# Reciprocal roots of the norms: logarithm and exponential of ScalarE replaced by a bit estimate and three Newton steps on VectorE

## The chip, the cores and the metric

One core of a Trainium2 chip runs the whole program: TensorE (PE), VectorE (DVE), ScalarE (ACT), GpSimd (POOL) and SyncE (SP), which issues nearly all transfers. The metric is the device time of one execution in microseconds (us); lower is better.

## The reference, cut to what matters

Two transformer blocks over 1024 tokens of width 1024, in float32. Every norm needs one reciprocal root for each token:

```python
def layer_norm(x, g, b):      # ln0 on the input, ln1 after the mixer, ln2 after the feed-forward block
    mu = xf.mean(-1, keepdims=True)
    var = jnp.square(xf - mu).mean(-1, keepdims=True)
    return ((xf - mu) * lax.rsqrt(var + EPS) * g + b)
def rmsnorm(x, g):            # norm_mix, norm_cross, norm_mem, norm_mlp, norm_final
    return xf * lax.rsqrt(jnp.mean(xf * xf, axis=-1, keepdims=True) + NORM_EPS) * g

x = layer_norm(x, ln0_g, ln0_b); mod = silu(c) @ w_ada + b_ada
y = hybrid_mixer(h, ...)                                # ends in @ w_o
x = layer_norm(ALPHA * x + (1.0 + gt_a) * y, ln1)
y = conv_ffn(h, ...)                                    # up, convolution, silu gate, down
x = layer_norm(ALPHA * x + (1.0 + gt_f) * y, ln2)
h = h + concat(attn, rec)(rmsnorm(h, norm_mix)) @ w_out
h = h + memory_cross_attention(rmsnorm(h, norm_cross), rmsnorm(mem, norm_mem), ...)   # ends in @ w_co
h = h + square(relu(rmsnorm(h, norm_mlp) @ w_mlp_in)) @ w_mlp_out
out = rmsnorm(h, norm_final)
```

## The kernel before, in words

The tokens lie in eight tiles of 128 rows; `resid` holds them. A list of units (`schedule`) is written once, and every engine walks through the whole list in that order and does its own part of each unit. Each engine therefore has one queue whose order is the order of the list. Between engines there are only named waits on semaphores: an instruction that waits stops everything behind it on its engine, whether or not that needs the same value. Where a unit has no part on an engine, the engine passes it at once.

A norm of a group of tiles is `norm_start`: for each tile `moments` (VectorE, the layer norms `s` = 0, 1, 2) or `squares` (ScalarE, the others), and then one unit `deviation` for the group. `deviation` turns the variances, one column for each tile (so 2, 3, 4 or 8 columns of 128 rows), into the reciprocal roots `rstd`. VectorE writes variance plus EPS (L1576, counted as "var"), ScalarE waits for it and does `Ln` (L2290) and `Exp` with scale -0.5 (L2292), VectorE waits for that and does one Newton step in four small instructions (L1579, L1581, L1583, L1585). There are 17 such units. After them come the users: `norm_apply` on VectorE (L1601 for ln1; L1605 and L1609 for ln2) or on ScalarE (L2337 writes `xhat`), `final` (L2342 on ScalarE, then L1658 on VectorE and the store), the transposes of `norm_features` (L1092 on TensorE) and their evictions (L1639, L1646, L1631 on VectorE, L2305 and L2314 on ScalarE). Of ln2, GpSimd adds the bias row (L2709), which is counted as `rows_added`.

Where other work stands near a `deviation`, in the order of the list:

- After the last group of `w_o` (tiles 6 and 7): `deviation(1, 6)`, then the product with `w_ada` for the second gate in eight steps (L1068), its copies `ada_out` on ScalarE (L2362, tile `mod_last`), its turn on TensorE (L1080), then `ahead`, at which ScalarE takes the first three panels of the feed-forward weights apart (`halve`, L2253, after the panel has landed) and GpSimd makes their low parts (`lower`, L2639), then the features of tiles 6 and 7, of which GpSimd makes the odd low parts, and then `up`.
- At the end of `down`: `deviation(2, 0)`, `squares` of the memory tokens (L2328 on `mem_t`), `deviation(norm_mem)`, the eight last evictions of `down` (L1979), the memory's features, `ck` (L1438, copied by ScalarE at L2582) with the first tiles' `norm_apply` between, the moments of tiles 4 to 7, `deviation(2, 4)`, `ck(2)`, `squares` of norm_mix for tiles 0 to 3, `deviation(norm_mix, 0)`, `norm_apply` of ln2 for tiles 4 to 7 (L1605, L1609), `cv`, and the features of tiles 0 to 3 (L1092, L1646). A softplus of eight columns (`rg_params`: L1752 on VectorE, `Exp` L2393 and `Ln` L2395 on ScalarE) stands before `ck`.
- `norm_cross` in `w_out`, `norm_mlp` in `w_co` (three groups each, with features of one group between the products of the next), and `norm_final` behind the last two halves of `mlp_out`.

ScalarE's functions live in tables that an instruction ACT_TABLE_LOAD brings in; it stands before the wait of the function that needs it. Copy and Square appear in the trace without a load of their own.

The tiles `panel_hi` (three buffers) share addresses with `xhat` 0 and 1, whose last readers before the feed-forward block are the transposes of tiles 4 and 5 and `norm_scale_rows` of tile 5 (L1615, `rows_applied`). Weights go through six slots, loaded in order by SyncE as the slots come free (L2836).

Of the kernel before, what the change touches and what calls it, by code (L numbers as in the profile page):

```python
# [8 lines left out]
I32 = mybir.dt.int32  # L9
ALU = mybir.AluOpType  # L10
ACT = mybir.ActivationFunctionType
# [4 lines left out]
D = 1024  # L16
KD = D // P
T = 1024
NT = T // P
HALVES = T // BANK  # L20
EPS = 1e-6
# [1471 lines left out]
def vector_program(k):  # L1493
    dve = k.nc.vector
    v = Program(k, dve)
# [71 lines left out]
    def deviation(s, n0, n1):  # L1567
        centred = s in (0, 1, 2)
        if centred:
            v.wait_ge("moments", s, n1 - 1)  # L1570
        else:
            v.wait_ge("squares", s, n1 - 1)
        cols = slice(n0 + NT, n1 + NT) if s == "norm_mem" else slice(n0, n1)
        var = k.moments[:, cols, 1 if centred else 0]
        x, y, step = k.newton[:, 0, cols], k.rstd[:, cols], k.newton[:, 1, cols]
        dve.tensor_scalar(x, var, 1.0 if centred else 1.0 / D, EPS, ALU.mult, ALU.add).then_inc(  # L1576
            *v.new("deviation_dve", s, n0, "var"))
        v.wait_ge("deviation_act", s, n0, "exp")
        dve.tensor_tensor(step, y, y, ALU.mult).then_inc(*v.new("deviation_dve", s, n0, 1))  # L1579
        v.wait_ge("deviation_dve", s, n0, 1)  # L1580
        dve.tensor_tensor(step, step, x, ALU.mult).then_inc(*v.new("deviation_dve", s, n0, 2))  # L1581
        v.wait_ge("deviation_dve", s, n0, 2)
        dve.tensor_scalar(step, step, -0.5, 1.5, ALU.mult, ALU.add).then_inc(*v.new("deviation_dve", s, n0, 3))  # L1583
        v.wait_ge("deviation_dve", s, n0, 3)
        dve.tensor_tensor(y, y, step, ALU.mult).then_inc(*v.new("deviation_dve", s, n0, 4))  # L1585
        v.wait_ge("deviation_dve", s, n0, 4)

    def ln0_norm(n):
        dve.tensor_scalar(k.xhat0[:, n, :], k.x_in[:, n, :], k.moments[:, n, 0:1], k.rstd[:, n:n + 1], ALU.subtract,
# [624 lines left out]
    def mlp_out(i, u, h, p, tiles):  # L2214
        for n in tiles:
            v.wait_ge(*v.filled("mlp_out", i, u, h, n))
            if u or i:
# [4 lines left out]
    v.run(dict(norm_scale_rows=norm_scale_rows, unit_length=unit_length, barrier=barrier, constants=constants, vectors=vectors, ada_turn=ada_turn, piece_out=piece_out, ln0_norm=ln0_norm,  # L2222
               ln0_resid=ln0_resid, gla_start=gla_start, z_gate=z_gate, gg_gate=gg_gate,
               modulation=modulation, norm_rows=norm_rows, moments=moments, deviation=deviation, norm_apply=norm_apply,
               norm_features=norm_features, final=final, project=project, to_tokens=to_tokens, decay_gates=decay_gates,
               delta_start=delta_start, delta=delta, gla_gates=gla_gates, gla=gla, ffn_taps=ffn_taps, up=up, down=down,
# [7 lines left out]
def scalar_program(k):  # L2234
    act = k.nc.scalar
    a = Program(k, act)
# [3 lines left out]
    def halve(p):  # L2240

        at = k.split_index[p]
        if at >= SPLITS:
            a.wait_ge(*k.released(a, splits[at - SPLITS]))
        if k.panel_list[p][3] is not None:
            a.wait_ge("panel_scaled", p)
        else:
            a.wait_ge("panel_loaded%d" % (p % SLOTS), p)
        if k.panel_list[p][0] == "up":
            for c in range(4):  # L2250
                for h in range(HALVES):
                    a.wait_ge("z_gated", c, h)
        act.activation(k.halves_of(p)[0], k.view(p), ACT.Copy).then_inc(*a.new("halved_hi", p))  # L2253

    def before(index, used):
        if used is None or not k.panel_list[used][2]:
            return
        while split_turn[0] < len(splits) and split_turn[0] <= k.split_index[used] + SPLITS - 1 and \
                same_group(k, splits[split_turn[0]], used) and k.passed(splits[split_turn[0]], SPLITS, index) and \
                k.passed(splits[split_turn[0]], None, index):  # L2260
            halve(splits[split_turn[0]])
            split_turn[0] += 1
# [18 lines left out]
    def condition():  # L2281
        for n in range(k.n_vt):
            a.wait_ge(*a.evicted("vectors", n))
        act.activation(k.cond[:], k.col("c", 0, KD), ACT.Silu).then_inc(*a.new("condition_silu"))

    def deviation(s, n0, n1):
        cols = slice(n0 + NT, n1 + NT) if s == "norm_mem" else slice(n0, n1)
        x, y = k.newton[:, 0, cols], k.rstd[:, cols]
        a.wait_ge("deviation_dve", s, n0, "var")
        act.activation(y, x, ACT.Ln).then_inc(*a.new("deviation_act", s, n0, "ln"))  # L2290
        a.wait_ge("deviation_act", s, n0, "ln")
        act.activation(y, y, ACT.Exp, scale=-0.5).then_inc(*a.new("deviation_act", s, n0, "exp"))  # L2292

    def norm_features(s, tiles, chunks):
        cols = slice(tiles[0] * P, (tiles[-1] + 1) * P)
# [302 lines left out]
    def mlp_in(i, c, h, p):  # L2598
# [4 lines left out]
        if i:  # L2603
# [2 lines left out]
        act.activation(k.mlp_hid[c][0][:, half(h)], k.mlp_sq[h][:], ACT.Copy).then_inc(*a.new("mlp_hi", i, c, h))  # L2606

    a.run(dict(unit_length=unit_length, barrier=barrier, vectors=vectors, condition=condition, ada_out=ada_out, conv_silu=conv_silu,
               piece_out=piece_out, z_gate=z_gate, gg_gate=gg_gate, rab=rab, deviation=deviation, squares=squares,
               norm_apply=norm_apply, norm_features=norm_features, final=final, project=project, decay_gates=decay_gates, delta=delta, gla_gates=gla_gates, gla=gla,  # L2610
               up=up, rg_params=rg_params, rg_in=rg_in, rglru=rglru, masks=masks, weights=weights, turn=turn,
               merge=merge, out_turn=out_turn, ck=ck, c_score=c_score, c_finish=c_finish, mlp_in=mlp_in))
# [382 lines left out]
def build(nc, dram, known):  # L2995
    with ExitStack() as stack:
        k = Shared(nc, dram, known, stack)
        sync_program(k)
        tensor_program(k)
        vector_program(k)  # L3000
        scalar_program(k)
        gpsimd_program(k)
        return k.signals.seen
# [35 lines left out]
```

## Time and profile before

| what | value |
|---|---|
| median of 3 runs | 3252.06 us (3250.96 to 3254.82) |
| the profiled execution | 3255.33 us, of which 3254.1 us are the span of its instructions |
| TensorE busy | 3083.5 us (95%) |
| VectorE, ScalarE, GpSimd busy | 1450.2, 963.9 and 734.8 us |
| mean granted clock of TensorE | 0.978 |

Busy time is a sum over the span and says nothing of order; what sets the end is read from the chain that ended last and from the timeline. In rows of a timeline the first number is the start in us from the span's start, the second the time from there to the end of the merged instructions, and the square bracket is how long the engine had been idle and who released it.

### The profile page before, as it was taken

How to read it: one execution, taken by the hardware profiler on the slowest of the kernel's cores; microseconds unless marked ns; L12 is line 12 of the kernel's file. 1: busy time of each engine (PE TensorE's matmuls, PEld its weight loads, DVE VectorE, ACT ScalarE, POOL GpSimd, SP SyncE). 2: the span in 40 equal slices, each digit the busy share in tenths (PEclk: the TensorE clock that was granted, in tenths of full speed). 3: DMA queues.
4: the chain of work that ended last, by engine and by line, in shares of the span. 5: the costliest groups of instructions: out<-in, count | busy, mean ns of one | idle time of the engine just before them, and what ended most of it. 6: DMA issues, size and time to landing. Idle time of an engine off the chain costs nothing.

```text
span 3254.1 us, 31713 instructions
## 1 busy us (share of the span) xinstructions
PE 3083.5 (95%) x12748; PEld 2101.5 (65%) x12748; DVE 1450.2 (45%) x2248; ACT 963.9 (30%) x1516; POOL 734.8 (23%) x467
## 2 busy tenths in 40 slices
PE   6999999999979999999987999999998999999997
PEld 3444467675437888888864444586443788888886
DVE  7245443332555545455555544673132333333334
ACT  2246622223022222222224540263334322222123
POOL 3011012220234444444432111100000122222220
PEclk9999999999989999999998999999999999999998
DMA  7210012213231111111122112002301111111111
GB/s 254 65 27 25 26 48 77 64 28 115 97 103 52 59 52 46 46 52 46 46 65 65 39 38 62 19 3 62 102 26 33 35 50 46 52 46 52 46 52 52
DMA packets 197649, 185.12 MB, mean 57 GB/s; under 512 B 16103, under 2 KB 147583, under 8 KB 197503
## 3 DMA queue, kind: packets, MB, share of 16 engines
q1 hardware_dynamic: 196928, 182.89, 18.0%
q8 instruction: 102, 1.67, 0.2%
q14 instruction: 44, 0.36, 0.0%
q10 hardware_dynamic: 575, 0.20, 0.0%
HBM read 171.24 MB, written 9.70 MB: 56 GB/s over the span
## 4 chain that ended last, share of the span: by engine, by line
PE 84%; DVE 7%; ACT 6%; issue 1%; POOL 1%; DMA 1%; ACTq 0%; DVEq 0%; SPq 0%; POOLq 0%
PE bank L1099 63%; PE bank L1125 6%; PE bank L1419 2%; PE bank L1189 1%; PE bank L1230 1%; PE bank L1244 1%; PE bank L1092 1%; PE bank L1253 1%; PE bank L1403 1%; PE bank L1068 1%; PE bank L1373 1%; PE bank L1395 1%; DVE ffn_conv L1968 1%; DVE ffn_conv L1964 1%; PE bank L1392 1%
## 5 line engine op out<-in xcount | busy, mean ns | idle before, releaser
L1099 PE MATMUL bank<-ft,panel 128*128 128x512 f32 x832 | 361.2, 595 | 1.8 <-ACT sq_inv L2457 1.0
L2639 POOL TENSOR_TENSOR panel_lo<-panel,panelm_hi 128x1024 fp32r<-128x1024 f32 x64 | 153.2, 2394 | 812.1 <-ACT panelm_hi L2253 812.1
L1099 PEld LDWEIGHTS bank<-ft,panel 128*128 128x128 f32 x832 | 158.4, 191 | 201.2 <-issue 201.2
L1125 PE MATMUL bank<-ft,panel 128*128 128x512 f32 x576 | 271.6, 609 | 7.4 <-ACT mod_part L2362 4.8
L1099 PE MATMUL bank<-ft_hi,panel_lo 128*128 128x512 f32 x704 | 277.4, 394 | 0.0
L1099 PE MATMUL bank<-ft_hi,panel_hi 128*128 128x512 f32 x704 | 276.5, 393 | 0.0
L1099 PE MATMUL bank<-ft_lo,panel_hi 128*128 128x512 f32 x704 | 276.3, 393 | 0.0
L1964 DVE TENSOR_SCALAR ffn_conv<-ffn_in,ffn_taps 128x512 f32<-128x512 f32 x88 | 115.4, 1312 | 296.3 <-ACT ffn_in L2502 296.3
L2220 DVE TENSOR_TENSOR resid<-resid,bank 128x512 f32<-128x512 f32 x256 | 174.5, 686 | 151.6 <-PE bank L1099 150.7
L2639 POOL TENSOR_TENSOR panel_lo<-panel,panel_hi 128x1024 fp32r<-128x1024 f32 x66 | 158.1, 2404 | 251.2 <-ACT panel_hi L2253 251.2
L1099 PE MATMUL bank<-ftm_hi,panelm_hi 128*128 128x512 f32 x512 | 200.5, 392 | 0.0
L1099 PE MATMUL bank<-ftm_lo,panelm_hi 128*128 128x512 f32 x512 | 200.1, 391 | 0.0
L1099 PE MATMUL bank<-ftm_hi,panel_lo 128*128 128x512 f32 x512 | 199.9, 390 | 0.0
L1099 PE MATMUL bank<-panelm_hi,mlp_hid_hi 128*128 128x512 f32 x512 | 199.2, 389 | 0.0
L1099 PE MATMUL bank<-panel_lo,mlp_hid_hi 128*128 128x512 f32 x512 | 199.2, 389 | 0.0
L1099 PE MATMUL bank<-panelm_hi,mlp_hid_lo 128*128 128x512 f32 x512 | 199.2, 389 | 0.0
L1125 PEld LDWEIGHTS bank<-ft,panel 128*128 128x128 f32 x576 | 105.3, 194 | 114.0 <-issue 110.8
L1099 PE MATMUL bank<-panel,mix 128*128 128x512 f32 x384 | 168.6, 596 | 0.9 <-DVE mix L2199 0.9
L1968 DVE SCALAR_TENSOR_TENSOR ffn_conv<-ffn_in,ffn_taps,ffn_conv 128x512 f32<-128x512 f32 x176 | 156.5, 889 | 6.2
L1099 PEld LDWEIGHTS bank<-ft_lo,panel_hi 128*128 128x128 f32 x704 | 132.6, 188 | 30.9
L1099 PEld LDWEIGHTS bank<-ft_hi,panel_hi 128*128 128x128 f32 x704 | 132.6, 188 | 29.6
L1099 PEld LDWEIGHTS bank<-ft_hi,panel_lo 128*128 128x128 f32 x704 | 132.6, 188 | 29.4
(421 smaller groups left out, 5325.1 us busy)
## 6 DMA issues: line engine op xcount, KB each, us to landing
panel<-in_w_in SPq DMA_DIRECT2D x52, 512.0 KB, 3.7
panel<-in_w_ada SPq DMA_DIRECT2D x48, 512.0 KB, 3.9
panel<-in_ffn_w_up SPq DMA_DIRECT2D x44, 512.0 KB, 3.7
panel<-in_w_mlp_in SPq DMA_DIRECT2D x32, 512.0 KB, 3.9
panel<-in_w_mlp_out SPq DMA_DIRECT2D x32, 512.0 KB, 3.5
panel<-in_w_o SPq DMA_DIRECT2D x24, 512.0 KB, 3.5
panel<-in_w_out SPq DMA_DIRECT2D x24, 512.0 KB, 3.5
panel<-in_ffn_w_down SPq DMA_DIRECT2D x22, 512.0 KB, 3.5
```

What stands on the lines that cost most here:

```text
L1068: m = te.matmul(ps[rows, :], k.cond[:, c:c + 1].broadcast_to([P, 32]), w[:, kk, :], start=(c < 4), stop=(c >= 4))
L1092: m = te.transpose(ps[:, tile(i)], src[:, tile(j)], k.ident[:])
L1099: m = te.matmul(ps, a, b, start=(start and j == 0), stop=(stop and j == len(pairs) - 1))
L1125: m = te.matmul(ps[:], w[0][:, kk, :], k.ft[:, kk, half(h)], start=(kk == 0), stop=(kk == KD - 1))
L1189: m = te.matmul(ps[:, tile(h)], lhs(h), rhs_of(h), start=True, stop=True)
L1230: m = te.matmul(ps[:, h * GC:(h + 1) * GC], t.ltm[:, h, :], blocks(t.inv, lv, 0)[:, h], start=True, stop=True)
L1244: m = te.matmul(ps[:, h * GC:(h + 1) * GC], t.prod[:, h, :], blocks(t.inv_t, lv, 1)[:, h], start=True, stop=True)
L1419: m = te.matmul(ps[:, at:at + HD + 1], k.p_t[(2 * t + hb) % 4][:, 2 * side + c, :], v, start=(hb == side == c == 0), stop=(hb == side == c ...
L1964: dve.tensor_scalar(out, pre[:, 1 + h * BANK:1 + (h + 1) * BANK], w[:, 0:1], w[:, 3:4], ALU.mult, ALU.add).then_inc(*v.new("ffn_tap", c, g ...
L1968: dve.scalar_tensor_tensor(out, pre[:, 1 + j + h * BANK:1 + j + (h + 1) * BANK], w[:, j:j + 1], out, ALU.mult, ALU.add).then_inc(*v.new("f ...
L2220: evict(dve.tensor_tensor(r, r, v.bank("mlp_out", i, u, h, n)[:], ALU.add), "mlp_out", i, u, h, n)
L2639: pool.tensor_tensor(lo, k.view(p), hi.bitcast(F32), ALU.subtract).then_inc(*g.new("halved_lo", p))
```

## The change

ScalarE's part of `deviation` is gone. VectorE makes the whole of it: the variance, its word shifted right by one, the first estimate as a constant minus that word (both on int32 views of the same tiles), and then three Newton steps of three instructions, each of which counts a semaphore and is waited for by the next. The last still counts as `("deviation_dve", s, n0, 4)`, which the users wait for. ScalarE's `halve` gets two named waits for the panels of `up`: the last transposes of tiles 4 and 5, and `rows_applied` of tile 5.

```diff
-        dve.tensor_scalar(x, var, 1.0 if centred else 1.0 / D, EPS, ALU.mult, ALU.add).then_inc(
-            *v.new("deviation_dve", s, n0, "var"))
-        v.wait_ge("deviation_act", s, n0, "exp")
-        dve.tensor_tensor(step, y, y, ALU.mult).then_inc(*v.new("deviation_dve", s, n0, 1))
...
-        dve.tensor_tensor(y, y, step, ALU.mult).then_inc(*v.new("deviation_dve", s, n0, 4))
-        v.wait_ge("deviation_dve", s, n0, 4)
+        def did(ins, *what):
+            ins.then_inc(*v.new("deviation_dve", s, n0, *what))
+            v.wait_ge("deviation_dve", s, n0, *what)
+        did(dve.tensor_scalar(x, var, 1.0 if centred else 1.0 / D, EPS, ALU.mult, ALU.add), "var")
+        did(dve.tensor_scalar(step.bitcast(I32), x.bitcast(I32), 1, None, ALU.logical_shift_right), "halved")
+        did(dve.tensor_scalar(y.bitcast(I32), step.bitcast(I32), -1.0, float(0x5F3759DF), ALU.mult, ALU.add), "first")
+        for n in range(1, 4):
+            did(dve.scalar_tensor_tensor(step, y, -0.5, y, ALU.mult, ALU.mult), "square", n)
+            did(dve.tensor_tensor(step, step, x, ALU.mult), "product", n)
+            did(dve.scalar_tensor_tensor(y, step, 1.5, y, ALU.add, ALU.mult), *(("step", n) if n < 3 else (4,)))
...
                 for h in range(HALVES):
                     a.wait_ge("z_gated", c, h)
+            a.wait_ge(*a.filled("feat", 1, 4, KD - 1))
+            a.wait_ge("rows_applied", 1, 5)
...
-    def deviation(s, n0, n1):
-        cols = slice(n0 + NT, n1 + NT) if s == "norm_mem" else slice(n0, n1)
-        x, y = k.newton[:, 0, cols], k.rstd[:, cols]
-        a.wait_ge("deviation_dve", s, n0, "var")
-        act.activation(y, x, ACT.Ln).then_inc(*a.new("deviation_act", s, n0, "ln"))
-        a.wait_ge("deviation_act", s, n0, "ln")
-        act.activation(y, y, ACT.Exp, scale=-0.5).then_inc(*a.new("deviation_act", s, n0, "exp"))
```

## Rows read from the trace of the kernel before

**Rows 1.** The page, part 4: the chain that ended last, by engine.
```profile
PE 84%; DVE 7%; ACT 6%; issue 1%; POOL 1%; DMA 1%; ACTq 0%; DVEq 0%; SPq 0%; POOLq 0%
```

**Rows 2.** ScalarE's groups by line: xcount | busy us, mean ns | idle before.
```profile
L2292 ACT ACT_TABLE_LOAD x17 | 21.8, 1283 | 0.3
L2290 ACT ACT_TABLE_LOAD x16 | 20.5, 1283 | 0.3
```

**Rows 3.** Timeline of the last 31 us, both groups of norm_final.
```profile
3223.34 0.17 DVE L1576 TENSOR_SCALAR newton<-moments 128x4 f32<-128x4 f32 x1 [1.27 <-ACT square L2328]
...
3228.41 4.63 DVE L1658 TENSOR_TENSOR resid<-resid,norm_rows 128x1024 f32<-128x1024 f32 x4 [1.27 <-ACT resid L2342]
...
3232.96 4.87 DVE L2220 TENSOR_TENSOR resid<-resid,bank 128x512 f32<-128x512 f32 x8
...
3241.08 0.17 DVE L1576 TENSOR_SCALAR newton<-moments 128x4 f32<-128x4 f32 x1 [3.26 <-ACT square L2328]
...
3244.12 0.16 DVE L1579 TENSOR_TENSOR newton<-rstd 128x4 f32<-128x4 f32 x1 [2.86 <-ACT rstd L2292]
...
3244.91 4.27 ACT L2342 ACTIVATE resid<-resid,rstd 128x1024 f32<-128x1024 f32 x4 [0.83 <-DVE rstd L1585]
```

**Rows 4.** VectorE's timeline: one instruction on int32 words, one small two-operation form.
```profile
54.95 0.43 DVE L2093 TENSOR_SCALAR dist_i<-dist_i 128x512 int32<-128x512 int32 x1
...
1711.96 0.17 DVE L1752 SCALAR_TENSOR_TENSOR lam<-lam_sp,lam 128x8 f32<-128x8 f32 x1
```

**Rows 5.** Timeline from 931 to 953 us, end of w_o: SyncE, ScalarE, VectorE, TensorE, GpSimd.
```profile
931.60 0.47 SPq L2836 DMA_DIRECT2D panel<-in_ffn_w_up  x1
...
938.52 0.20 ACT L2290 ACTIVATE rstd<-newton 128x2 f32<-128x2 f32 x1 [13.16 <-DVE newton L1576]
...
944.92 2.95 ACT L2253 ACTIVATE panel_hi<-panel 128x1024 fp32r<-128x1024 f32 x3
...
938.32 0.17 DVE L1576 TENSOR_SCALAR newton<-moments 128x2 f32<-128x2 f32 x1
...
941.06 1.53 DVE L1601 TENSOR_SCALAR xhat<-resid,moments,rstd 128x1024 f32<-128x1024 f32 x2
...
940.76 2.07 PE L1080 MATMUL bank<-mod_last,quads 128*128 128x512 f32 x2 [6.11 <-ACT mod_last L2362]
...
946.05 7.15 POOL L2639 TENSOR_TENSOR panel_lo<-panel,panel_hi 128x1024 fp32r<-128x1024 f32 x3 [14.20 <-ACT panel_hi L2253]
```

**Rows 6.** Transfers issued from 930 to 931.7 us: KB each, us to landing.
```profile
panel<-in_ffn_w_up SPq DMA_DIRECT2D x1, 512.0 KB, 7.9
```

**Rows 7.** Timeline from 1682 to 1765 us: SyncE, ScalarE, VectorE, GpSimd, TensorE.
```profile
1682.63 0.37 SPq L2978 DMA_DIRECT2D mem_t<-in_mem  x1
...
1697.11 0.21 ACT L2290 ACTIVATE rstd<-newton 128x4 f32<-128x4 f32 x1 [14.57 <-DVE newton L1576]
...
1698.74 1.04 ACT L2328 ACTIVATE square<-mem_t 128x1024 f32<-128x1024 f32 x1
...
1704.91 4.87 DVE L1979 TENSOR_TENSOR resid<-resid,bank 128x512 f32<-128x512 f32 x8
...
1745.00 0.81 DVE L1605 TENSOR_SCALAR resid<-resid,moments,rstd 128x1024 f32<-128x1024 f32 x1
...
1728.59 2.36 POOL L2709 TENSOR_TENSOR resid<-resid,norm_rows 128x1024 f32<-128x1024 f32 x1 [1.16 <-DVE resid L1609]
...
1761.02 3.68 PE L1092 MATMUL bank<-ident,xhat 128*128 128x128 f32 x16 [8.66 <-DVE ft L1646]
```

**Rows 8.** Transfers issued from 1680 to 1700 us.
```profile
mem_t<-in_mem SPq DMA_DIRECT2D x1, 1024.0 KB, 4.9
```

**Rows 9.** Chain of waits from 2255 to 2390 us (w_out, norm_cross), by line.
```profile
by line: PE bank L1099 94.1%; PE bank L1092 5.2%; DVE ft L1646 0.7%; issue 0.1%; DVEq L93 0.0%
```

**Rows 10.** TensorE's timeline in w_co, behind norm_mlp's second unit.
```profile
2495.70 1.97 PE L1092 MATMUL bank<-ident,xhat 128*128 128x128 f32 x8 [5.74 <-DVE ftm_lo L1631]
```

**Rows 11.** Stretch by engine: us, busy (instructions) of five engines, PEclk, DMA share, GB/s.
```profile
2496.00:2498.00 2.00, 2.00 (x9) 1.80 (x8) 0.66 (x2) 0.98 (x2) 0.00 (x0) 0.50 0.00 0
```

More of the change, by code:

```diff
@@ L1575, in deviation @@
         x, y, step = k.newton[:, 0, cols], k.rstd[:, cols], k.newton[:, 1, cols]
-        dve.tensor_scalar(x, var, 1.0 if centred else 1.0 / D, EPS, ALU.mult, ALU.add).then_inc(
-            *v.new("deviation_dve", s, n0, "var"))
-        v.wait_ge("deviation_act", s, n0, "exp")
-        dve.tensor_tensor(step, y, y, ALU.mult).then_inc(*v.new("deviation_dve", s, n0, 1))
[L1580 to L1584, printed above, removed]
-        dve.tensor_tensor(y, y, step, ALU.mult).then_inc(*v.new("deviation_dve", s, n0, 4))
-        v.wait_ge("deviation_dve", s, n0, 4)
+        def did(ins, *what):
[8 more added lines that the diff above has]
+            did(dve.scalar_tensor_tensor(y, step, 1.5, y, ALU.add, ALU.mult), *(("step", n) if n < 3 else (4,)))
     def ln0_norm(n):
@@ L2608, in scalar_program @@
     a.run(dict(unit_length=unit_length, barrier=barrier, vectors=vectors, condition=condition, ada_out=ada_out, conv_silu=conv_silu,
-               piece_out=piece_out, z_gate=z_gate, gg_gate=gg_gate, rab=rab, deviation=deviation, squares=squares,
+               piece_out=piece_out, z_gate=z_gate, gg_gate=gg_gate, rab=rab, squares=squares,
                norm_apply=norm_apply, norm_features=norm_features, final=final, project=project, decay_gates=decay_gates, delta=delta, gla_gates=gla_gates, gla=gla,
```

## The prediction

> **What bounds the kernel now.** I read the page's chain of waits first: TensorE holds 84% of it, VectorE 7% and ScalarE 6% [rows 1]. So most of the time is products, and the change can win only in the stretches where TensorE stands still for a norm. The second view is ScalarE's groups by line, for the number of table loads: 16 for `Ln`, 17 for `Exp`, 1.283 us each [rows 2], so two for nearly each of the 17 units. Third, the timeline around every `deviation`, to see two things: how long VectorE takes from the variance (L1576) to the first user, and what stands behind ScalarE's wait in its queue. Fourth, the chain in each stretch, for whether a norm is on it at all.
>
> The 17 units fall into two kinds. In nine of the eleven norms that ScalarE's squares feed, ScalarE is busy until the variance is ready and both loads are exposed: from L1576 to the first user 3244.91 - 3241.08 = 3.83 us [rows 3] (the other two of the eleven, norm_mem and the first of norm_mix, take nearly the same, since their squares too end just before). In those fed by VectorE's moments (six; ln0, with eight columns and its `Ln` table late, lies between) ScalarE has waited idle, has its `Ln` table in already, and the way takes 941.06 - 938.32 = 2.74 us [rows 5].
>
> **Part 1: the new sequence.** Twelve small dependent instructions on VectorE. The pitch of dependent small ones is (3244.91 - 3244.12)/4 = 0.20 us, with the wait between them in it [rows 3]. The kinds: a two-operation form with three operands on eight columns takes 0.17 us, as the others do [rows 4]. A form on int32 words has no small row; 512 columns take 0.43 us [rows 4], so for 2 to 8 columns it lies between 0.20 (the small float ones) and 0.43. I take 0.20, as the instruction is of the same kind and only the columns differ. Sum 12 x 0.20 = 2.40 us; with the upper bound for two of them 2.86. Against 3.83 that is a gain of 1.43 us (bounds 0.97 to 1.43; nothing below 0.20 is likely, as each waits for the one before), against 2.74 a gain of 0.34 (bounds -0.12 to 0.34). I call these the long and the short gain.
>
> The Trainium skill, page "VectorE: DVE Perf Modes", section "The DRAIN you can't avoid", says that chaining does not help, that the next instruction waits for the pipeline to empty, and that one should make the count of instructions small. That speaks against going from five to twelve. By its formula for a float two-input instruction, (N+151)/0.96 ns (same page, errata section), twelve would make an estimated 1.94 us before any gap; the trace's 0.20 us pitch is what I use, and by either the count costs less than the loads give back.
>
> **Part 2: where the gain is on the path.** ln0: the chain there runs over transfers of `w_ada` and TensorE alone; gain 0, the cover is those transfers. norm_cross, three units: the chain from 2255 to 2390 us holds TensorE for 99% and no norm [rows 9]; gain 0, the next group's products hide it, and without them it would be 1.43 each. norm_mlp, three units: the first lies under products, but behind the second TensorE stands 5.74 us until VectorE evicts a transpose (L1631), which is queued behind `deviation` [rows 10], and behind the third the pattern repeats (5.9 us). ScalarE's half of that eviction also stood behind the loads and comes earlier still. Gain 2 x 1.43 = 2.9 us. norm_final, two units: in the first, the users L1658 hold VectorE until 3232.96, when the eight last evictions start, all but the last of whose banks TensorE has long filled; they in turn set the second squares. So both units are in the chain, the second with nothing beside it [rows 3]. Gain 2 x 1.43 = 2.9 us.
>
> **Part 3: what stood behind ScalarE's waits.** This is the larger part. ScalarE waited in five units for VectorE's variance. Two places have other work behind that.
>
> (a) End of `w_o`. The first two groups of ln1 are short ones on the chain, 2 x 0.34 = 0.7 us. In the third ScalarE waits 13.16 us until 938.52 [rows 5]. Behind it stands the copy `mod_last`, whose input is older than TensorE's last work before it stops at 940.76 - 6.11 = 934.65; TensorE is idle from there to 940.76 for that copy [rows 5]. Then come the second copy and the three `panel_hi` (944.92), and GpSimd's three `panel_lo` (946.05, 7.15 us), behind which its part of the features is queued and for that TensorE [rows 5]. With the wait gone, TensorE turns the first half at about 934.7 (1.0 us at full clock), the last two steps of the product are done at about 938.5, as their panels land at about 937, and the second copy ends at about 939. Late next is the first `up` panel: issued at 931.60 and 7.9 us on the way, so 939.5 [rows 5, 6]. One `panel_hi` is 2.95/3 = 1.0 us, so GpSimd starts at 940.6 instead of 946.05, and with the 0.7 us of the groups before at 939.9. The place gives 6.1, say 6.0 us in all. Bounds: 1.0 us if the copy is not what holds it (three short gains), 7 if the panels land sooner. VectorE's own way (`xhat` 941.06 + 1.53, the two gate rows and `feat_part`, now shifted to about 943.3) ends before GpSimd's (947.1), so it is covered. The new waits of `halve` name things that are long done: GpSimd adds tile 5's row after L1615, which stands behind that group's features in VectorE's queue, and GpSimd was through with it at 946.05 - 14.20 = 931.85 [rows 5], over 7 us before the first `panel_hi` can start. They cost nothing; if they did, ScalarE's features of tiles 6 and 7 behind them would be late next.
>
> (b) End of `down`. ScalarE waits 14.57 us until 1697.11, does `Ln` and `Exp`, and only then, at 1698.74, the squares of `mem_t` [rows 7], though the memory landed at 1682.63 + 0.4 + 4.9 = 1687.9 [rows 7, 8]. Without the wait these are done by about 1690.5 (two of 1.25), and on VectorE the two units follow each other: 1696.9 + 2.4 + 2.4 = 1701.7. The eight evictions L1979 then start at 1701.7 instead of 1704.91: 3.2 us [rows 7]. After that the softplus: its `Exp` found its table in, left by the norm; now the silu table is in and a load of 1.28 us comes before it, of which ScalarE's idle 1.0 us hides most. Cost 0.3 us, so 2.9 us remain. The same pattern stands at 1734.2, 2 of 2 here: ScalarE waits 13.5 us for ln2's second group, and the four squares of norm_mix for tiles 0 to 3 follow only from 1736.3. Their inputs are complete with GpSimd's L2709 at 1728.59 + 2.36 = 1730.95, now 1728.1 [rows 7]; the last square, 1.25 us, ends at 1729.3, before VectorE's ln2 variance at 1731.3. So VectorE does the two units back to back, 1731.3 + 2.4 + 2.4 = 1736.1, and L1605 starts there instead of at 1745.00: 8.9 us [rows 7]. From L1605 to TensorE's transposes at 1761.02, for which TensorE had stood 8.66 us on VectorE's `ft`, is one queue of VectorE [rows 7], so TensorE goes on 8.9 us sooner. TensorE's `cv`, itself 3 us sooner, ends at about 1738, in time. The second norm_mix unit is hidden by the products of `rg` and gives 0. Bounds: 3.5 us (two long and two short gains) if the squares don't run ahead, 9.6 with the softplus free.
>
> **Part 4: loads.** 33 loads leave ScalarE. Of them the exposed ones are counted above. A few later functions now bring a table in themselves (the softplus above); the first silu of the feed-forward block loses its load. The Trainium skill, page "ScalarE: Activation LUTs", section "What ACT_TABLE_LOAD costs", gives 1283 ns for the load and about 1380 ns of drain on top for every switch. The trace agrees on the first [rows 2] and shows no drain: `Ln` starts at 1.28 us behind its load. By the page's 2.66 us a long unit would have lasted over 6 us, and it lasts 3.83.
>
> **Sum.** (a) 6.0 + (b) 8.9 + norm_mlp 2.9 + norm_final 2.9 = 20.7 us. The profiled execution goes from 3255.33 to 3234.6, and the median, 3.3 us lower, from 3252.06 to 3231.4 us (0.64%). A measurement of this kernel tells about 0.2%, 6.5 us, from no change.
>
> **The rivals.**
> 1. Only the latencies count: the work behind ScalarE's waits is held by something else (the panels' landing, GpSimd, banks). Then (a) gives 1.0 and (b) 3.5, the sum is 1.0 + 3.5 + 5.8 = 10.3 and the time 3242. For it: in (a) 3 MB of panels are in flight. Against it: the rows put the released work's inputs 6 to 10 us ahead. Between it and the forecast lie the cases with one of the two places whole. Together 0.22.
> 2. No change, within 6.5 us: the gains are absorbed by feed-forward and later products, which wait for panels. Against: TensorE's waits name VectorE and ScalarE, not a transfer, except at `w_ada`. 0.05.
> 3. Slower: the instructions on int32 words are slow in the small form. To decide, the long units (mlp, final: 4) and the pairs in (b) would have to lose the 20.7 us; with 11 units on the path that is 1.9 us for each unit, 0.95 us for each of two instructions over the 0.20 us. At 1.5 us each the sum is 20.7 - 11 x 2.6 = -8 us, 3260 us. Against it: 0.43 us for 512 columns [rows 4]. 0.03.
> The forecast has 0.70.
>
> **Clock.** TensorE's granted clock falls in these waits: behind the 5.74 us of rows 10 it is 0.50, the lower level of 1.2 GHz, for the products from 2496 to 2498 [rows 11], against 0.978 in the mean. I count no gain from it, as 4.3 us of that wait stay (5.74 - 1.43). Where a fall is avoided, products of some 3 to 4 us take half, an estimate of 1.5 us a place, for three places about 5 us. This sets the lower end: 3226. The upper end reaches past rival 1 to 3243. Faster 0.92, same 0.05, slower 0.03.
>
> **What the profile after would show.** No ACT_TABLE_LOAD under `deviation`; L1576 to the first user 2.4 us everywhere; `mod_last` before 935 and `panel_lo` before 941; squares of `mem_t` at 1688 less the shift, L1979 and L1605 3 and 9 us sooner relative to the last product of `down`'s first half; norm_cross without effect; from the last matmul to the end 2.8 us less. Wrong it would be if a panel or GpSimd, not ScalarE's queue, ends TensorE's wait in (a), or if the last L2220 waits for TensorE.

## The result, and the profile after

The changed kernel takes 3236.98 us in the median of 6 runs (3233.82 to 3239.71), the kernel before 3253.44 us in 6 runs beside them. The ratio is 0.9947, with a 95% interval of 0.9937 to 0.9957: 17.2 us less by the ratio (16.5 by the medians), where 20.7 had been forecast. The predicted time was 3231.4, its range 3226 to 3243. The profiled execution took 3237.97 us with a span of 3236.7.

**The new sequence.** VectorE's timeline of the kernel after, last unit of norm_final, which answers to [rows 3], with ScalarE's first user of the root at the end:

```profile
3225.16 0.17 DVE L1583 TENSOR_SCALAR newton<-moments 128x4 f32<-128x4 f32 x1 [3.26 <-ACT square L2325]
3225.36 0.17 DVE L1584 TENSOR_SCALAR newton<-newton 128x4 int32<-128x4 int32 x1
3225.57 0.17 DVE L1585 TENSOR_SCALAR rstd<-newton 128x4 int32<-128x4 int32 x1
3225.77 0.16 DVE L1587 SCALAR_TENSOR_TENSOR newton<-rstd 128x4 f32<-128x4 f32 x1
...
3227.35 0.16 DVE L1589 SCALAR_TENSOR_TENSOR rstd<-newton,rstd 128x4 f32<-128x4 f32 x1
...
3227.55 4.27 ACT L2339 ACTIVATE resid<-resid,rstd 128x1024 f32<-128x1024 f32 x4 [2.42 <-DVE rstd L1589]
```

Read the starts: they are 0.20 us apart, also from one instruction on int32 words to the next. From the variance to the first user it is 3227.55 - 3225.16 = 2.39 us, before 3.83. The two-sided question on the int32 form (0.20 or up to 0.43) is settled at the lower end. ScalarE loads 102 tables in place of 136.

**End of w_o.** Timeline of the kernel after, 931 to 955 us, the rows that answer to [rows 5]: ScalarE, VectorE, GpSimd, TensorE:

```profile
931.26 0.59 ACT L2359 COPY mod_last<-bank 128x512 f32<-128x512 f32 x1 [7.54 <-PE bank L1068]
938.77 0.59 ACT L2359 COPY mod_last<-bank 128x512 f32<-128x512 f32 x1 [6.93 <-PE bank L1068]
939.25 1.06 ACT L2258 ACTIVATE panel_hi<-panel 128x1024 fp32r<-128x1024 f32 x1
940.62 1.06 ACT L2258 ACTIVATE panel_hi<-panel 128x1024 fp32r<-128x1024 f32 x1 [0.30 <-DMA panel<-in_ffn_w_up]
...
937.98 0.17 DVE L1583 TENSOR_SCALAR newton<-moments 128x2 f32<-128x2 f32 x1
...
940.36 5.67 DVE L1604 TENSOR_SCALAR xhat<-resid,moments,rstd 128x1024 f32<-128x1024 f32 x2
945.95 2.37 DVE L1950 COPY ffn_taps<-cols 128x132 f32<-128x132 f32 x1
...
949.56 0.98 DVE L1642 TENSOR_SCALAR feat_part<-bank,in_scale,in_bias 128x256 f32<-128x256 f32 x2
...
940.39 7.84 POOL L2636 TENSOR_TENSOR panel_lo<-panel,panel_hi 128x1024 fp32r<-128x1024 f32 x3 [8.87 <-ACT panel_hi L2258]
951.07 0.72 POOL L2715 TENSOR_TENSOR ft_lo<-feat_part,ft_hi 128x256 fp32r<-128x256 f32 x1 [2.83 <-ACT ft_hi L2302]
...
954.74 0.78 PE L1099 MATMUL bank<-ft_hi,panel_hi 128*128 128x512 f32 x1
```

ScalarE does what was forecast: the copy goes ahead of the norm, and the panels' high parts follow as they land. GpSimd starts its low parts at 940.39, 5.66 us sooner than in [rows 5], or 5.3 us when both are measured from the variance. But VectorE's two `xhat` instructions, which started within 0.03 us of it, now take 5.67 us in place of 1.53, and the copy of the taps behind them 2.37. So the features come late, GpSimd waits 2.83 us for them, and `up` starts 16.76 us behind the variance, where it was 18.52.

**End of down.** The same timeline, 1684 to 1750 us (ScalarE, VectorE, TensorE), for [rows 7]:

```profile
1684.69 1.06 ACT L2325 ACTIVATE square<-mem_t 128x1024 f32<-128x1024 f32 x1 [6.41 <-DMA mem_t<-in_mem]
...
1705.73 1.28 ACT L2390 ACT_TABLE_LOAD   x1
...
1725.92 1.06 ACT L2325 ACTIVATE square<-resid 128x1024 f32<-128x1024 f32 x1 [2.36 <-POOL resid L2706]
...
1699.84 4.87 DVE L1982 TENSOR_TENSOR resid<-resid,bank 128x512 f32<-128x512 f32 x8
...
1749.93 3.68 PE L1092 MATMUL bank<-ident,xhat 128*128 128x128 f32 x16 [8.88 <-DVE ft L1649]
```

The squares of `mem_t` now stand right behind their transfer, 14 us sooner than in [rows 7] (12.2 us measured from ln2's variance), and those of norm_mix are done at 1727.1, before ln2's variance at 1729.13. The softplus brings its own table in (L2390), as foreseen.

**Where the time came from.** Each column is the time in us from one instruction to the next: `g0` to `g2` are the variances of ln1's three groups, `up` is TensorE's first product of it, `2a` and `2b` are ln2's variances, `mix` the second one of norm_mix, `cross` the first of norm_cross, `m1` to `m3` those of norm_mlp, `f1` and `f2` those of norm_final. The numbers at the left are those of the experiments below. It is worked out from the starts of L1583 (L1576 with the logarithm) and of L1099 in the profiled executions of this and the later kernels:

```
              start   g0-g1  g1-g2  g2-up   up-2a  2a-2b 2b-mix mix-cross cross-m1 m1-m2 m2-m3  m3-f1  f1-f2 f2-end
before       862.27   41.73  34.32  18.52  740.06  37.28  36.04   502.60   204.52 13.73 25.39  706.88  17.74  13.01
after        864.52   39.67  33.79  16.76  740.34  34.05  29.99   502.77   204.51 13.73 23.06  705.67  16.30  11.58
5 again      860.69   39.67  33.76  16.57  740.44  34.05  29.99   502.81   204.52 13.73 23.07  705.67  16.31  11.57
1 wait all   862.92   39.66  33.77  19.50  739.21  36.74  34.93   500.52   204.51 13.73 25.08  706.73  16.31  11.56
2 wait ln1   863.30   39.66  33.78  19.50  739.24  34.24  29.98   500.52   204.51 13.73 23.28  705.80  16.31  11.55
3 hold       862.99   39.66  33.77  14.86  740.11  34.23  29.98   500.52   204.53 13.73 23.42  705.94  16.30  11.58
4 hold,first 857.83   41.36  34.22  10.47  740.55  34.05  29.98   502.65   204.51 13.74 24.68  706.88  16.30  11.56
6 two steps  863.19   39.07  33.50  16.22  739.37  32.89  28.54   500.53   204.51 13.73 22.69  705.62  15.71  10.98
7 five steps 862.82   42.28  34.36  17.90  739.94  36.74  32.37   502.97   204.52 13.73 25.45  706.90  17.49  12.77
8 4 and 6    861.89   39.07  33.36   9.88  740.72  32.89  28.81   502.16   204.51 13.74 24.15  706.73  15.72  10.98
9 bef,first  862.51   40.03  33.77  14.94  739.77  37.30  36.04   502.55   204.51 13.73 25.37  706.84  17.75  13.03
```

From the first variance of ln1 to the end it is 3254.1 - 862.27 = 2391.8 us before and 2372.2 after: 19.6 us less. The first 860 us, in which little is changed, differ from one execution to the next by up to 6.7 us (857.8 to 864.5), and with them one profiled time from another. So the 17.2 us of the ratio (interval 14.0 to 20.5) and the stretches' 19.6 us do not contradict each other.

### The profile page after: what moved, and what is told of

Same layout as the page of the kernel before. It is cut to its first block, busy times and chain, and to the rows that moved or that the text cites. A ratio compares the mean times of both kernels' runs of the same rounds, so it can differ in the third digit from the quotient of the medians.

```text
span 3236.7 us, 31765 instructions
## 1 busy us (share of the span) xinstructions
PE 3081.1 (95%) x12748; PEld 2099.1 (65%) x12748; DVE 1475.7 (46%) x2367; ACT 913.9 (28%) x1448; POOL 735.5 (23%) x467
## 4 chain that ended last, share of the span: by engine, by line
PE 85%; DVE 7%; ACT 4%; issue 1%; DMA 1%; POOL 1%; SPq 0%; ACTq 0%; DVEq 0%; POOLq 0%
PE bank L1099 63%; PE bank L1125 6%; PE bank L1419 2%; PE bank L1189 1%; PE bank L1230 1%; PE bank L1244 1%; PE bank L1253 1%; PE bank L1403 1%; PE bank L1092 1%; PE bank L1373 1%; PE bank L1068 1%; PE bank L1395 1%; DVE ffn_conv L1971 1%; DVE ffn_conv L1967 1%; PE bank L1392 1%
## 5 line engine op out<-in xcount | busy, mean ns | idle before, releaser
L1099 PE MATMUL bank<-ft,panel 128*128 128x512 f32 x832 | 361.4, 595 | 1.8 <-ACT sq_inv L2454 1.0
L1099 PEld LDWEIGHTS bank<-ft,panel 128*128 128x128 f32 x832 | 158.5, 191 | 201.4 <-issue 201.4
L1099 PE MATMUL bank<-ft_hi,panel_lo 128*128 128x512 f32 x704 | 277.0, 393 | 0.0
L1099 PE MATMUL bank<-ft_hi,panel_hi 128*128 128x512 f32 x704 | 276.3, 392 | 0.0
L1099 PE MATMUL bank<-ft_lo,panel_hi 128*128 128x512 f32 x704 | 276.0, 392 | 0.0
L1099 PE MATMUL bank<-ftm_hi,panelm_hi 128*128 128x512 f32 x512 | 200.7, 392 | 0.0
L1099 PE MATMUL bank<-ftm_lo,panelm_hi 128*128 128x512 f32 x512 | 200.2, 391 | 0.0
L1099 PE MATMUL bank<-ftm_hi,panel_lo 128*128 128x512 f32 x512 | 200.1, 391 | 0.0
L1099 PE MATMUL bank<-panelm_hi,mlp_hid_hi 128*128 128x512 f32 x512 | 199.2, 389 | 0.0
L1099 PE MATMUL bank<-panel_lo,mlp_hid_hi 128*128 128x512 f32 x512 | 199.2, 389 | 0.0
L1099 PE MATMUL bank<-panelm_hi,mlp_hid_lo 128*128 128x512 f32 x512 | 199.2, 389 | 0.0
L1099 PE MATMUL bank<-panel,mix 128*128 128x512 f32 x384 | 167.7, 594 | 0.9 <-DVE mix L2202 0.9
L1099 PEld LDWEIGHTS bank<-ft_lo,panel_hi 128*128 128x128 f32 x704 | 132.4, 188 | 30.8
L2210 DVE TENSOR_TENSOR mlp_square<-mlp_act 128x512 f32<-128x512 f32 x64 | 44.3, 692 | 235.7 <-ACT mlp_act L2599 235.7
L1099 PEld LDWEIGHTS bank<-ft_hi,panel_lo 128*128 128x128 f32 x704 | 132.4, 188 | 29.4
```

Source lines behind the costliest of these rows:

```text
L1099: m = te.matmul(ps, a, b, start=(start and j == 0), stop=(stop and j == len(pairs) - 1))
L2210: dve.tensor_tensor(k.mlp_sq[h][:], k.mlp_act[h][:], k.mlp_act[h][:], ALU.mult).then_inc(*v.new("mlp_square", i, c, h))
```

## The experiments

**1. ScalarE waits again, in all norms.** It has its unit back, with a wait for the finished root and nothing else. The latency stays new, what stands behind the wait is held again.

```diff
+    def deviation(s, n0, n1):
+        a.wait_ge("deviation_dve", s, n0, 4)
```

> The changed kernel, with ScalarE again waiting in every norm until VectorE's reciprocal root is there (the last Newton step), but computing nothing. It parts the latency of the norms from what stands behind ScalarE's waits. The prediction's terms: the end of w_o falls from 6.0 to 1.0 us and the end of down from 8.9 to 3.5, so +10.4 us against the changed kernel's 3237, 3247. Read from the changed kernel's trace, where the third group of ln1 brought less than forecast, I expect +5.4 at the end of down and +2 to +3 at the end of w_o, so 3244 to 3246. Rival 1 (only the latencies count): no difference, 3237.

Measured: 3248.79 us, ratio 0.9982 (0.9973 to 0.9991), 11.4 us above the changed kernel by the two ratios, and more than the 3244 to 3246 us expected. Without what stood behind the waits some 6 us of the 17 are left (up to 1.7 us more, as the waits here end later, see below), and rival 1 falls. ScalarE's timeline of this kernel:

```profile
938.72 0.59 ACT L2362 COPY mod_last<-bank 128x512 f32<-128x512 f32 x1 [16.64 <-DVE rstd L1589]
...
1697.45 1.06 ACT L2328 ACTIVATE square<-mem_t 128x1024 f32<-128x1024 f32 x1 [17.77 <-DVE rstd L1589]
```

Both waits name the root, not data. In the table the end of down loses 2.69 + 4.94 = 7.6 us, not 5.4, and g2-up 2.7 to 2.9. Part of this is that the wait is for the last step, 2.4 us behind the variance, while before the squares of `mem_t` started 1.84 us behind it (1698.74 - 1696.90). That is 0.56 us for each of two pairs of norms, so about 6.5 of the 7.6 us are the queue's. TensorE's wait behind the second norm_mlp was 5.12 us in place of 4.29, too: ScalarE's half of the features counted there.

**2. The wait in ln1 alone.** As 1, with `if s == 1:` ahead of the wait.

> As the kernel before this one, but ScalarE waits in the three groups of ln1 alone. The prediction's term for the end of w_o: +5.0 us, 3242. By the changed kernel's trace, where up's first product came 16.8 us behind the variance and before the change 18.5: +2.3 us (the copy mod_last again 2.4 us behind the variance), 3239. If the place gave nothing through the queue: 3237. The end of down stays as in the changed kernel.

Measured: 3238.84 us, ratio 0.9951 (0.9939 to 0.9964). The time alone can't tell 2 us from none. The stretch can: g2-up is 19.50 as in 1, against 16.76 and 16.57, and all of 2a to mix stays as in the changed kernel. So freeing ScalarE at the end of w_o gives 2.8 us in the kernel as changed, not 5.3, and some 0.56 us of the 2.8 may again be the later end of this wait. The two places are independent of each other.

**3. GpSimd's first low part waits for VectorE's last `xhat`.**

```diff
         g.wait_ge("halved_hi", p)
+        if p == min(q for q, x in enumerate(k.panel_list) if x[0] == "up"):
+            g.wait_ge("normed", 1, 7)
         pool.tensor_tensor(lo, k.view(p), hi.bitcast(F32), ALU.subtract)...
```

> The changed kernel, but GpSimd starts the first up panel's low part only when VectorE has normalised tile 7. Theory (VectorE's float32 work from SBUF to SBUF stands still while GpSimd computes): the two xhat instructions take 1.5 us again instead of 5.67, the copy of the taps 0.23 instead of 2.37 or what of GpSimd still meets it, feat_part starts at about 944 instead of 949.56, GpSimd goes from its last panel_lo to ft_lo without the wait of 2.83, and up starts 1.3 to 2.8 us sooner in the stretch; total 3234 to 3236. Rival (VectorE is slowed by something else there, the transfers of the panels or ScalarE): xhat keeps 5.7 us, up starts up to 1.5 us later, 3237 to 3238.5.

Measured: 3236.2 us, ratio 0.9941 (0.9927 to 0.9954); the time alone can't tell this kernel from the changed one. VectorE and GpSimd of this kernel:

```profile
938.79 1.54 DVE L1604 TENSOR_SCALAR xhat<-resid,moments,rstd 128x1024 f32<-128x1024 f32 x2
940.25 0.23 DVE L1950 COPY ffn_taps<-cols 128x132 f32<-128x132 f32 x1
...
940.48 7.17 POOL L2638 TENSOR_TENSOR panel_lo<-panel,panel_hi 128x1024 fp32r<-128x1024 f32 x3 [10.51 <-DVE xhat L1604]
947.61 0.72 POOL L2717 TENSOR_TENSOR ft_lo<-feat_part,ft_hi 128x256 fp32r<-128x256 f32 x1
```

The same transfers are in flight and ScalarE does the same work beside it; only GpSimd is held. `xhat` has its 1.5 us back, the copy its 0.23, GpSimd goes on to the features without a wait, and `up` starts 14.86 us behind the variance although GpSimd began 1.7 us later relative to it. So it is GpSimd's work beside it that makes `xhat` slow.

**4. Only the first panel's low part ahead of the features.** As 3, and:

```diff
-        while turn[0] < len(worked) and turn[0] <= worked.index(used) + SPLITS - 1 and \
+        more = 0 if k.order[index][0] == "ahead" else SPLITS - 1
+        while turn[0] < len(worked) and turn[0] <= worked.index(used) + more and \
```

> As the kernel before this one, and GpSimd makes only the first up panel's low part ahead of the features, the next two behind them. Theory: GpSimd is through with its panel at about 944.4, the features' low parts are then paced by VectorE and ScalarE (1.9 us a pair, four pairs), up's first product at about 948 to 950 instead of 954.74, minus 5 to 7 us in this stretch, if the second panel's low part is in time; total 3231 to 3233. Rival: the low parts that now come behind the features meet VectorE's and TensorE's work there, or the second panel is late, and half or all of it is given back: 3234 to 3237.

Measured: 3232.86 us, ratio 0.9932 (0.992 to 0.9945). GpSimd and TensorE of this kernel:

```profile
937.47 2.36 POOL L2638 TENSOR_TENSOR panel_lo<-panel,panel_hi 128x1024 fp32r<-128x1024 f32 x1 [10.51 <-DVE xhat L1604]
940.21 0.72 POOL L2718 TENSOR_TENSOR ft_lo<-feat_part,ft_hi 128x256 fp32r<-128x256 f32 x1 [0.38 <-ACT ft_hi L2302]
...
947.43 5.74 POOL L2638 TENSOR_TENSOR panel_lo<-panel,panel_hi 128x1024 fp32r<-128x1024 f32 x2
...
943.88 0.78 PE L1099 MATMUL bank<-ft_hi,panel_hi 128*128 128x512 f32 x1
...
950.86 0.50 PE L1099 MATMUL bank<-ft_hi,panel_hi 128*128 128x512 f32 x1 [0.24 <-POOL panel_lo L2638]
```

`up` starts 10.47 us behind the variance, 6.1 to 6.3 sooner than in the changed kernel, and the second panel costs 0.24 us. By the ratios 4.6 us of it arrive (0.9946 - 0.9932), with intervals of 0.0025. The table says that nothing is lost behind it: up-2a is 740.55, against 740.34 and 740.44. What this profiled execution loses against the changed kernel stands in stretches that its edit doesn't touch: g0-g1 (1.7 us more than in the changed kernel), g1-g2 (0.4), m2-m3 (1.6) and m3-f1 (1.2). Experiment 5 looks at these.

**5. The changed kernel again.** No edit.

> The changed kernel unaltered, once more. Every theory: 3235 to 3239, ratio 0.994 to 0.996. What it tells: how far the first 860 us of one execution differ from another's (they were 2.3 us longer in the changed kernel's profiled execution than in the one before the change), and how much the first eight products behind the second norm_mlp vary with the granted clock behind one and the same wait of 4.29 us (4.1 to 5.7 us so far).

Measured: 3236.99 us, ratio 0.9946 (0.9934 to 0.9959). In the table this execution agrees with the first to 0.2 us in every stretch, but its start is 3.8 us shorter. Inside g2-up the agreement hides a difference. Here GpSimd began 2.07 us behind the variance, not 2.41, and met the last Newton instruction, of two columns, before `xhat`:

```profile
936.29 2.26 DVE L1589 SCALAR_TENSOR_TENSOR rstd<-newton,rstd 128x2 f32<-128x2 f32 x1
...
936.19 7.39 POOL L2636 TENSOR_TENSOR panel_lo<-panel,panel_hi 128x1024 fp32r<-128x1024 f32 x3 [8.53 <-ACT panel_hi L2258]
```

It took 2.26 us in place of 0.16, so the root of this group was there 4.43 us behind the variance, not 2.34. The 2.3 us by which the changed kernel's start had been longer in its profile are no effect of the change that can be shown. TensorE's timeline behind the second norm_mlp, in the changed kernel (first execution):

```profile
2483.30 1.97 PE L1092 MATMUL bank<-ident,xhat 128*128 128x128 f32 x8 [4.29 <-DVE ftm_lo L1634]
2485.07 4.08 PE L1099 MATMUL bank<-panel,mix 128*128 128x512 f32 x8
```

The same place in experiment 3:

```profile
2477.55 1.91 PE L1092 MATMUL bank<-ident,xhat 128*128 128x128 f32 x8 [4.29 <-DVE ftm_lo L1634]
2479.25 4.51 PE L1099 MATMUL bank<-panel,mix 128*128 128x512 f32 x8
```

And in experiment 4:

```profile
2472.53 1.97 PE L1092 MATMUL bank<-ident,xhat 128*128 128x128 f32 x8 [4.29 <-DVE ftm_lo L1634]
2474.30 5.71 PE L1099 MATMUL bank<-panel,mix 128*128 128x512 f32 x8
```

Behind one and the same wait of 4.29 us the first eight products take 4.08, 4.51 and 5.71 us (4.30 in experiment 2, and in this second execution again 4.08 behind 4.30); the next eight take 3.60 in each. What the clock's lower level costs behind a wait thus differs by up to 1.6 us between kernels that are alike in this stretch. The stretch m3-f1 goes the same way: TensorE's wait in it is 4.46 us in the changed kernel and in experiment 4, yet it is 705.67 us in one and 706.88 in the other, which is what it was before the change.

**6. Two of Newton's steps.** `range(1, 4)` becomes `range(1, 3)`: three instructions less in each of the 17 units.

> The changed kernel with two of Newton's steps in place of three (the reciprocal root then good to about 5 in a million). 3 instructions less in every norm, 3 x 0.20 = 0.59 us. The prediction has 11 units on the path (three in ln1, ln2's first with norm_mem, ln2's second with norm_mix's first, two of norm_mlp, two of norm_final): -6.5 us, 3230.5. Rival: some of them are covered (the first two of ln1 by the next group's products, the pair ln2 and norm_mem by GpSimd): -3 to -4.5 us, 3233. norm_cross, ln0, the first norm_mlp and the second norm_mix: nothing.

Measured: 3227.52 us, ratio 0.9916 (0.9903 to 0.993), 9.8 us under the changed kernel by the ratios, with intervals that hold the 6.5 expected as well.

**7. Five of Newton's steps.** `range(1, 6)`: six more.

> The changed kernel with five of Newton's steps: 6 instructions more in every norm, 1.18 us. By the prediction's 11 units +13 us, 3250; if only 7 of them are on the path +8.3, 3245. The trace tells unit by unit: each stretch between two variances is longer by 1.18 times the units in it that are on the path, and those of norm_cross stay as they are.

Measured: 3251.27 us, ratio 0.9989 (0.9981 to 0.9998), 14 us above. One step has 3 x 0.197 = 0.59 us (1.18 for two). Against the changed kernel, 2a-2b grows by 2.69 and 2b-mix by 2.38 (two units each, 2.36), f1-f2 and f2-end by 1.2 each, and with two steps (experiment 6) g0-g1, f1-f2 and f2-end are 0.6 less each. cross-m1 and m1-m2 don't move at all.

Where the clock plays, the stretch is a poor witness (m3-f1 grows by 1.23, but beside experiment 4, with the same three steps, by 0.02), and TensorE's wait is a better one. With two, three and five steps it is 3.71, 4.29 and 5.47 us behind the second norm_mlp, 3.88, 4.46 and 5.64 behind the third, and 5.14, 5.73 and 6.91 behind ln1's second unit: the full step each time. That g1-g2 nevertheless grows by 0.57 to 0.60 only is the eight products behind this wait, which take 4.80 us here and 5.41 in the changed kernel.

ln1's third unit can't be read in this way. Its root takes much longer than five steps should:

```profile
941.83 2.21 DVE L1587 SCALAR_TENSOR_TENSOR newton<-rstd 128x2 f32<-128x2 f32 x1
944.07 2.27 DVE L1588 TENSOR_TENSOR newton<-newton 128x2 f32<-128x2 f32 x1
946.37 2.26 DVE L1589 SCALAR_TENSOR_TENSOR rstd<-newton,rstd 128x2 f32<-128x2 f32 x1
...
941.67 6.94 POOL L2636 TENSOR_TENSOR panel_lo<-panel,panel_hi 128x1024 fp32r<-128x1024 f32 x3 [8.68 <-ACT panel_hi L2258]
```

Three of the small instructions met GpSimd's three low parts, one each, and the first user started 9.80 us behind the variance in place of 3.58. Behind them `xhat` ran at its full pace, and so `up` started only 1.1 to 1.3 us later than in the changed kernel. That growth can't be booked for the two added steps.

So ten of the prediction's eleven units are on the path with their full length, and of the eleventh the runs don't tell. What the whole times show beyond 6.5 and 13.0 us stands in other stretches: in 6, up-2a is 1.0 us less (in 1 and 2 too) and mix-cross 2.2 us less (in 1, 2 and 3 too); in 7, g0-g1 has 1.4 and m2-m3 1.2 us more than the step. The 2.2 us of mix-cross are complete 12 us behind norm_mix's variance, in the products behind TensorE's long wait at the end of down. In the changed kernel and in experiment 2:

```profile
1754.47 16.21 PE L1099 MATMUL bank<-ft,panel 128*128 128x512 f32 x32 [0.87 <-ACT ft L2311]
```

```profile
1755.06 13.97 PE L1099 MATMUL bank<-ft,panel 128*128 128x512 f32 x32 [0.87 <-ACT ft L2311]
```

The granted clock is 0.50 from 1754 to 1759 us in the first and 1.00 from 1755 to 1759 in the second, behind waits of 8.88 and 10.06 us.

**8. Experiments 4 and 6 together.**

> GpSimd holds the first up panel's low part until tile 7 is normalised and makes only that one ahead of the features, as in the fourth kernel, and two of Newton's steps as in the sixth. The two act in different places, so they add: 3233 - 6.5 = 3226.5, if the kernels' gains are 3 us and 4.5 us, 3229. Were the gains of GpSimd's order lost again behind up, as much as the 6.3 us of its stretch stood beside 3.4 in the whole time: 3230.

Measured: 3223.4 us, ratio 0.9905 (0.9892 to 0.9919), the fastest of all: 31 us under the kernel before, and below the 3226.5 to 3230 expected. By the ratios the two edits add up within their intervals: experiments 4 and 6 alone give 0.0014 and 0.0030 over the changed kernel, together they give 0.0041. g2-up is 9.88. The root is that of experiment 6, so this version trades one Newton step for 0.59 us a unit; experiment 4 is the fastest with all three.

**9. The kernel before, with GpSimd's order alone.** The edit of 4 without the hold.

> The kernel before the change, with its logarithm and exponential, and of the later kernels only GpSimd's order: ahead of the features it makes the low part of the first up panel alone. Its first panel_lo starts at about 946 as before, behind VectorE's xhat, so no hold is needed. The features' low parts then follow from about 948.5 instead of 953.2, so up starts 4.6 us sooner, 13.9 us behind the variance instead of 18.5; total 3250 against 3254.5. If the gain of the order hangs on ScalarE being free, up starts less than 2 us sooner; if the place were held by ScalarE alone, as the prediction had it, nothing.

Measured: 3251.3 us, ratio 0.9991 (0.9982 to 1.0). `up` starts 14.94 us behind the variance in place of 18.52: 3.6 us, not 4.6. VectorE and GpSimd of this kernel:

```profile
945.60 0.69 DVE L1530 SCALAR_TENSOR_TENSOR gate_row<-bank,gate_row 128x512 f32<-128x512 f32 x1 [4.04 <-PE bank L1080]
...
944.47 2.36 POOL L2639 TENSOR_TENSOR panel_lo<-panel,panel_hi 128x1024 fp32r<-128x1024 f32 x1 [14.61 <-ACT panel_hi L2253]
947.73 0.72 POOL L2719 TENSOR_TENSOR ft_lo<-feat_part,ft_hi 128x256 fp32r<-128x256 f32 x1 [0.89 <-ACT ft_hi L2305]
```

The 0.89 us is most of what is missing: TensorE's turn of `mod_last` (L1080), still late through ScalarE's wait, holds VectorE's second gate row for 4.04 us, and behind it stand the features. With this the place is a square of four, in us from the variance to `up`: 18.52 before; 16.6 to 16.8 with ScalarE free; 14.94 with GpSimd's order; 10.47 with both and the hold of experiment 3 (the order without the hold was not run on the changed kernel). Where GpSimd does not stand in the way, the change is worth 14.94 - 10.47 = 4.5 us here, near the forecast's 5.3; where it does, 1.8 to 1.95.

## Why the prediction was right, and where it was off

**Part 1, the sequence: right.** 2.39 us, against 2.40; the units of norm_final gave 17.74 - 16.30 = 1.44 and 13.01 - 11.58 = 1.43, against 1.43 each. It holds only while GpSimd doesn't stand in the way: in experiments 5 and 7 it did, at ln1's third unit. Rival 3 (int32 forms slow) falls with the rows at 0.17 us.

**Part 2, where it is on the path: right.** norm_cross gave nothing (43.8 and 30.1 us between its groups, and 204.5 us from the first to norm_mlp, are the same before, after and with five steps). norm_mlp: TensorE's wait behind the second unit went from 5.74 to 4.29 us and behind the third from 5.91 to 4.46, 1.45 each, for 1.43. How much of it reaches the end of the stretch is up to the clock, see below.

**Part 3 (b), end of down: right in place and size.** Forecast 8.9 us; 2a-2b and 2b-mix gave 3.23 + 6.05 = 9.3. (The upper bound of 9.6 for this place does not follow from its terms: 8.9 and the 0.3 us of the softplus make 9.2.) The steps are there one by one: L1982 starts 4.76 us behind the variance, before 8.01, so 3.25 for the forecast's 3.2.

**Part 3 (a), end of w_o: mis-sized.** Of ln1's third group 5.3 us were forecast (6.0 less the 0.7 of the first two) and 1.8 to 1.95 came. The step that failed is the sentence that VectorE's own way ends before GpSimd's and so is covered. It took `xhat` at 1.53 us from a stretch in which GpSimd stood idle [rows 5], and moved GpSimd's start by 6 us onto it. The trace of the kernel before already had the sign, 10 us ahead of that `xhat`:

```profile
930.45 1.95 DVE L1731 TENSOR_TENSOR resid<-resid,gated 128x512 f32<-128x512 f32 x1
933.24 0.69 DVE L1731 TENSOR_TENSOR resid<-resid,gated 128x512 f32<-128x512 f32 x1
...
925.75 6.11 POOL L2709 TENSOR_TENSOR resid<-resid,norm_rows 128x1024 f32<-128x1024 f32 x2
```

The same instruction takes 1.95 us while GpSimd works, until 931.86, and 0.69 once it is done. ScalarE's steps ahead of `xhat`, and GpSimd's start at 940, came as worked out. Experiment 3 shows the collision as the cause, and gives back 1.8 of the 3.4 to 3.5 us that are missing. GpSimd's three low parts (7.2 us) ahead of the features were the second limit; experiment 4 takes them away.

**The new named wait: cost nothing visible.** `panel_hi` follows `mod_last` without a gap (939.25), and the two later gaps of 0.30 and 0.46 us name transfers.

**The clock: not in the sum, and it came in anyway.** The forecast counted no gain from it and used it for the lower end of the range alone, at an estimated 1.5 us a place. g0-g1 gave 2.06 us where 0.34 was forecast, and m2-m3 2.33 where 1.43 was. The difference, 1.7 and 0.9 us, is TensorE's lower level. It can't be booked for the change. In experiment 4, whose code is the changed kernel's there, both are gone again (41.36 and 24.68), and with them the 1.21 us of m3-f1 (706.88, as before). In experiment 9, whose code there is that of the kernel before, the 1.7 us of g0-g1 are there without the change (40.03). The first eight products of g0-g1 take 5.27 us before and 5.30 in 4, but 3.60 after and in 9. That the sum came so near is therefore in part luck: these 2.6 us hide most of the 3.5 us missing in (a): 20.7 forecast, less 3.5 in (a), plus 0.4 in (b), 1.9 in the first two groups of ln1 and 0.7 in norm_mlp, is 20.2; up-2a and mix-cross, with no norm on the path, took 0.45 of it, and the stretches' sum is 19.6.

**The chances.** Rival 1 (latencies alone) was given 10.3 us; experiment 1, its nearest test, has 6. Its mechanism is refuted at both places.

## What to carry to other kernels

An engine that waits in order for another's result is priced by what stands behind the wait, not by the two instructions that it does: here the queue was worth some 10 of 17 us. Before you move one engine's work earlier, list what it will then run beside, and take no duration from a stretch in which the neighbour stood idle; a freed queue can bring most when the next engine's order is changed with it. And with 0.2% between measurements, compare stretches between fixed instructions: here they repeat to 0.2 us, apart from those in which TensorE's clock fell. Where it fell, compare the wait itself.

## What the runs showed of the hardware

**VectorE and GpSimd hold each other up.** Each of the two `xhat` instructions (128x1024, float32, from SBUF to SBUF) took 2.82 to 2.93 us beside GpSimd's `panel_lo` and 0.81 without it (kernel before and experiment 3; the two records overlap by 0.08 us, so both together take 1.53), a factor of about 3.5. The view of the tile `xhat` in the kernel after, minimum, median and maximum in ns:

```profile
L1604 DVE TENSOR_SCALAR xhat<-resid,moments,rstd x2: 2824/2876/2928, 940.4 to 943.2; 128x1024 f32<-128x1024 f32 x2
```

Single records of GpSimd's first two low parts end at 942.74 and 945.48, those of the two `xhat` at 943.28 and 946.03. The copy of 132 columns took 2.37 us instead of 0.23, and ended at 948.32, within 0.1 us of GpSimd's last `panel_lo` (940.39 + 7.84 = 948.23). The Newton instructions of experiments 5 and 7, of two columns, took 2.21 to 2.27 us in place of 0.16. So what such an instruction loses does not go by its own size: it lasts until GpSimd's instruction is done. GpSimd lost less: 7.84 us for three in place of 7.17.

The Trainium skill, page "SBUF — State Buffer", section "Who interferes with whom", says that `tensor_scalar` and copies can enter a mode that takes the pair of ports shared with GpSimd, and that whoever starts second stands still for the whole instruction of the other. The ends, each with or just behind GpSimd's, agree with that. The trace has no record of the mode that an instruction ran in, and the order of the records does not settle who was first: that of the first `xhat` starts at 940.36, 0.03 us ahead of GpSimd's, and it was `xhat` that stood still.

**What TensorE's lower clock costs differs by some 2 us between like executions.** The granted clock falls to 0.50, the lower level of 1.2 GHz [rows 11], in waits of 3.7 to 10 us. The first eight products behind the waits of 3.7 to 5.7 us in norm_mlp take 4.1 to 5.8 us where 3.6 is full speed, and the 32 behind the long wait at the end of down 13.97 to 16.41. In g0-g1 it fell behind gaps of 0.3 to 0.5 us only, in the kernel before, and did not fall behind the same gaps in experiment 9. Kernels that are alike in a stretch fall on different sides, and which side one falls on was not traced to a cause here. So a gain or loss of up to 2 us at such a place in one profile tells nothing by itself.
